# Moving activations placed 32 bytes past a 64-byte boundary in a two-block model kernel

## The chip, the cores and the metric

The kernel runs as one program on one core of a Trainium2 chip. The metric is the device time of one execution in microseconds (us); less is better. All inputs lie in the chip's memory (HBM) at the start, and the output is written there.

## The reference, cut to what matters

Two blocks of two layers each run over 256 tokens of width 1024. The first block mixes an mLSTM and a retention, the second a convolution and a banded attention, followed by a dense feed-forward in layer 0 and eight experts in layer 1. The products with the large weights are what the change touches:

```python
p = h @ w_in[l]                                   # first block, 9 pieces a head, 4 heads
y = jnp.concatenate([y_m, y_r], -1) @ w_out[l]    # 2048 -> 1024
...
proj = h @ w_in_2[l]                              # second block
y = jnp.concatenate([y_conv, y_att], -1) @ w_out_2[l]
f = (jax.nn.silu(h @ w_gate) * (h @ w_up)) @ w_down            # layer 0: 1024 -> 2816 -> 1024
out = out + combine[:, e:e+1] * swiglu(t, w_gate[e], w_up[e], w_down[e])   # layer 1: 8 experts, 1024 -> 3584 -> 1024
```

All of it is float32, and the kernel keeps nearly that precision by splitting each operand into a high and a low part.

## The kernel before, in words

**Units.** The weights come in units of 1 MB: a tile of 128 partitions by 2048 float32. [...] TensorE then takes three products for each 128x128 piece: high weights with the high activations, high with low, low with high. `whi` and `wlo` have three slots each, `raw` has three or six.

**Which operand moves.** A matmul holds one operand in the array (the stationary one, brought by a weight load, at most 128 columns) and streams the other past it (the moving one). `mm(out, a, b)` holds `a` and moves `b`. In the first four stages the weights are stationary and 256 columns of activations move: `products` (L1127 to L1129) and `first_products` (L1144 to L1159) move `hhi` and `hlo`; `rows_product` (L1182 to L1184) moves the halves of y or of the feed-forward's activations (`yhi`/`ylo`, `y2hi`/`y2lo`, `fhi`/`flo`). `token_products` (L1168 to L1170) is the other way round: 128 columns of `hhi` or `hlo` are stationary and 256 columns of weights move. In the experts (L1641 to L1643 and L1670 to L1672) the tokens (`xghi`, `xglo`, `thi`, `tlo`) are stationary and 512 columns of weights move. The gates' sums (L1336 to L1338) hold 36 columns of `ghi` or `glo`, whose slices lie 144 bytes apart, and move `hhi` and `hlo`. Some small matmuls (norm sums L1199, means over a head L1282, scores, transposes) work on plain float32.

**Where tensors lie.** `sb(name, shape, ...)` takes memory in the order in which the program asks for it, and each tensor begins at the next multiple of 32 bytes (per partition) behind the one before. Several stages share one region: an `ExitStack` (`b1`, `b2`, `bf`, `bm`) is closed after its tensors are placed, and the next stage begins at the same address. Read from the built program, the byte address within a partition is a multiple of 64 for `raw`, `whi`, `wlo`, `h`, `hhi`, `hlo`, `yhi`, `ylo`, `y2hi`, `y2lo`, `fhi`, `flo`, `thi`, `tlo`, `xghi`, `xglo`, `pick`, `qpad`, `rot` and `ghi`. It is 32 past such a multiple for `ones`, `mean256`, `zacc`, `q2`, `v2`, `pT` and `mean512`. Slices of the large tensors begin at multiples of 512 bytes inside them.

**What sets the order.** Each engine's instructions are written out by hand and the engines wait for one another by semaphores; there is no scheduler. TensorE goes unit by unit. Beside the units of the first stages the kernel loads 1 MB pieces of the modulation weights (`ada`), which VectorE sums by itself (L1794); the sum's last step is on TensorE (L1211), and SP's next load of that kind waits for it.

Of the kernel before, what the change touches and what calls it, by code (L numbers as in the profile page):

```python
# [5 lines left out]
F32 = mybir.dt.float32  # L6
# [6 lines left out]
P = 128  # L13
# [45 lines left out]

UW = 2048
RAW = 6
HALF = 3
MOE_SLOTS = (3, 4, 5, 2, 0, 1)
# [11 lines left out]
HEAD_UNITS = 9  # L76
OUT1_UNITS = D_INNER * D // (P * UW)
MIX_UNITS = (2 * D_CONV + 3 * D_ATT) // 256
OUT2_UNITS = D * D // (P * UW)

# [16 lines left out]
S_MOE = S_B3 + UNIT_L2  # L97
assert S_MOE % HALF == 2 and A_MIX1 + ADA_MIX[1] == ADA_UNITS and (2 * HEAD_UNITS) % HALF == 0 and JOB_UNITS % RAW == 0 and JOB_UNITS % HL == 0 and ADA_TURN[0] % HALF == 0 and ADA_TURN[1] % HALF == 0
FREE0, DONE0 = HALF, 1
# [25 lines left out]
class Unit:  # L125
# [17 lines left out]
    @property  # L143
    def raw(self):
        return self.n % HALF if self.n < S_MOE else MOE_SLOTS[(self.n - S_MOE) % RAW]

    @property
    def loads(self):
        slots = HALF if self.n < S_MOE else RAW
        if self.n < S_MOE:  # L150
            first = self.n // HALF
        else:
            first = (self.n - S_MOE) // RAW + ((S_MOE + HALF - 1 - self.raw) // HALF if self.raw < HALF else ADA_UNITS // HALF - sum(HALF + i % HALF == self.raw for i in ADA_SPARE))
        return self.turn * (16 * self.per // slots) + (16 * first + 16) if self.per else 16 * first + 16
# [98 lines left out]
def two_block_model(nc, x, positions, consts, c, w_ada, b_ada, norm_g, w_in, conv_w, conv_b, b_igate, b_fgate,  # L253
# [7 lines left out]
    with ctx:  # L261
        def sb(name, shape, dt=F32, stack=ctx):
            return stack.enter_context(nc.sbuf_tensor(name, shape, dt))

        def sem(name):
            return ctx.enter_context(nc.semaphore(name))

        raw = sb("raw", [P, RAW, UW])
        whi = sb("whi", [P, HL, UW], F32R)  # L270
        wlo = sb("wlo", [P, HL, UW], F32R)
        xT = sb("xT", [P, KD, S])
        h = sb("h", [P, KD, S])
        hhi = sb("hhi", [P, KD, S], F32R)
        hlo = sb("hlo", [P, KD, S], F32R)
        cst = sb("cst", [P, C_BEFORE])
        ones = sb("ones", [P, S])
        mean256 = sb("mean256", [P, P])
# [11 lines left out]
        rstd = sb("rstd", [P, S])  # L290
        acc = sb("acc", [P, HALF, S])
        acc2 = sb("acc2", [P, S])

        b1 = ExitStack()
# [44 lines left out]
        sb("before_ylo", [P, D_INNER // P * S], F32, by)  # L340
        spare = sb("spare", [P, 2, UW], F32, by)
        by.close()
# [38 lines left out]

        bm = ExitStack()
        thi = sb("thi", [P, FE // P, P], F32R, bm)
        tlo = sb("tlo", [P, FE // P, P], F32R, bm)
        htok = sb("htok", [P, 2, D], F32, bm)
# [36 lines left out]

        raw_in = [sem(f"raw_in{i}") for i in range(RAW)]
        c_in, rows1_in = sem("c_in"), sem("rows1_in")
# [2090 lines left out]
```

How the kernel before makes its waits and increments, by code:

```python
    def wait(self, back=0):  # L240
        v = self.n - back
        self.eng.wait_ge(self.sem, self.turn * self.per + v if self.per else v)
# [254 lines left out]
        @block.sync  # L497
# [6 lines left out]
            def load(u, src, k):  # L504
                sp.wait_ge(raw_free, u.free(1 - (HALF if u.n < S_MOE else RAW)))
                sp.dma_start(raw[:, u.raw, :].rearrange("p (k n) -> p k n", k=k), src).then_inc(raw_in[u.raw], 16)
# [1 line left out]
            def ada_load(a, block, l, at):  # L509
                if a.n >= ADA_START:
                    sp.wait_ge(ada_done, a.count(1 - HALF))
                elif a.n >= HALF:
                    sp.wait_ge(ada_done, a.n - HALF - len(ADA_SPARE) + 1)
                w = (w_ada, w_ada_2)[block][l].rearrange("(k p) n -> p k n", p=P)
                sp.dma_start(raw[:, a.raw, :].rearrange("p (k n) -> p k n", k=KD), w[:, :, bass.ds(at * 256, 256)])\
                    .then_inc(raw_in[a.raw], 16)
# [58 lines left out]
                        w, c, half = (wg, wu)[j % 4 // 2], j // 4, j % 2  # L575
                        load(u, w[:, 4 * half:4 * half + 4, 512 * c:512 * c + 512], 4)
                    else:
                        f = 2 * (j - JOB_UP)
                        load(u, wd[:, f:f + 2, :], 2)
            sp.wait_ge(ada_done, ADA_UNITS)
            with sp.Fori(0, NE) as e:
                job_loads(e, e, S_MOE, range(JOB_UNITS))
            sp.wait_ge(jobs_ready, 1)
            nx = sp.value_load(jobs[0:1, 0:1], min_val=0, max_val=3)
            with sp.If(nx > 0):
                with sp.Fori(0, nx) as j:
```

## Time and profile before

| | us |
|---|---|
| median of 3 runs | 2150.38 (2146.89 to 2151.61) |
| the profiled execution, device time | 2151.25 |
| its span in the trace | 2149.4 |
| TensorE busy (PE) | 2096.3 |
| VectorE busy (DVE) | 1753.4 |
| ScalarE busy (ACT) | 1321.3 |

The profiled execution is 0.9 us above the median, and 1.9 us of it lie outside its span. On TensorE the start of a matmul is recorded and its end is modelled, and matmuls overlap in the pipeline; the time from the start of one to the start of the next (its spacing) is what a stream of them costs. The busy time of PE only says that something was under way.

### The profile page before, as it was taken

To read this page: it belongs to the slowest core of one execution; us is meant where nothing else is said; L and a number is where in the kernel's file an instruction comes from. 1 tells how busy PE (TensorE), PEld (TensorE's weight loads), DVE (VectorE), ACT (ScalarE), POOL (GpSimd) and SP (SyncE) were. 2 spreads that over 40 slices of the span, in tenths; PEclk is the share of its full clock that TensorE was granted. 3 is DMA by queue.
4 is the path that set the end of the run, shared out by engine and by line. 5 is a ranking of instruction groups with operands and counts; after the bars stand their busy time and mean duration, and the time that the engine had idled before them with its cause. 6 is when DMAs were issued, how large, how long until landed. Compare 5 with 4: busy or idle time off the path is not lost.

```text
span 2149.4 us, 33810 instructions
## 1 busy us (share of the span) xinstructions
PE 2096.3 (98%) x13585; PEld 1866.9 (87%) x13585; DVE 1753.4 (82%) x2161; ACT 1321.3 (61%) x1265; POOL 30.9 (1%) x60
## 2 busy tenths in 40 slices
PE   7999999999999999999999999999999999999998
PEld 5899999899999889999987888888888888888887
DVE  3978875877767878887877988888888888889887
ACT  3565554566645753434656777777777677776775
POOL 3000000000000000000000000000000000000000
PEclk8999999999999999999998999999999999999999
DMA  9777855666656548987545999999999999999995
GB/s 318 239 218 226 247 188 163 198 191 213 184 189 223 189 138 281 288 303 265 177 170 205 369 353 347 374 358 343 361 350 380 345 345 357 362 366 344 360 348 197
DMA packets 356161, 595.07 MB, mean 277 GB/s; under 512 B 10376, under 2 KB 201368, under 8 KB 356008
## 3 DMA queue, kind: packets, MB, share of 16 engines
q1 hardware_dynamic: 352864, 586.92, 79.1%
q0 software_dynamic: 2752, 5.86, 1.2%
q8 instruction: 110, 1.80, 0.3%
q14 instruction: 43, 0.35, 0.0%
q10 hardware_dynamic: 392, 0.13, 0.0%
HBM read 591.80 MB, written 4.22 MB: 277 GB/s over the span
## 4 chain that ended last, share of the span: by engine, by line
PE 82%; DVE 8%; DMA 3%; ACT 3%; issue 3%; SPq 0%; POOL 0%; DVEq 0%; POOLq 0%
PE ps L1641 9%; PE ps L1643 9%; PE ps L1642 9%; PE ps L1127 5%; PE ps L1128 5%; PE ps L1129 5%; PE ps L1670 5%; PE ps L1671 5%; PE ps L1672 5%; PE ps L1182 3%; PE ps L1183 3%; PE ps L1184 3%; DVE acc L1794 2%; DVE wlo L1738 2%; ACT whi L707 1%
## 5 line engine op out<-in xcount | busy, mean ns | idle before, releaser
L1738 DVE TENSOR_TENSOR wlo<-raw,whi 128x2048 fp32r<-128x2048 f32 x485 | 1109.0, 2288 | 264.9 <-ACT whi L707 249.5
L707 ACT CAST whi<-raw 128x2048 fp32r<-128x2048 f32 x485 | 926.0, 1909 | 389.0 <-PE ps L1643 133.7
L1127 PE MATMUL ps<-hhi,whi 128*128 128x256 f32 x1360 | 393.4, 289 | 0.2
L1128 PE MATMUL ps<-hlo,whi 128*128 128x256 f32 x1360 | 385.9, 284 | 0.0
L1129 PE MATMUL ps<-hhi,wlo 128*128 128x256 f32 x1360 | 385.8, 284 | 0.0
L1641 PE MATMUL ps<-whi,xghi 128*128 128x512 f32 x896 | 360.4, 402 | 0.8 <-DVE wlo L1738 0.8
L1643 PE MATMUL ps<-wlo,xghi 128*128 128x512 f32 x896 | 350.1, 391 | 0.0
L1642 PE MATMUL ps<-whi,xglo 128*128 128x512 f32 x896 | 349.0, 390 | 0.0
L1127 PEld LDWEIGHTS ps<-hhi,whi 128*128 128x128 f32 x1360 | 262.1, 193 | 7.3 <-issue 7.0
L1128 PEld LDWEIGHTS ps<-hlo,whi 128*128 128x128 f32 x1360 | 262.1, 193 | 0.3
L1129 PEld LDWEIGHTS ps<-hhi,wlo 128*128 128x128 f32 x1360 | 261.9, 193 | 0.0
L1643 PEld LDWEIGHTS ps<-wlo,xghi 128*128 128x128 f32 x896 | 168.2, 188 | 36.7
L1641 PEld LDWEIGHTS ps<-whi,xghi 128*128 128x128 f32 x896 | 168.3, 188 | 34.2 <-DVE wlo L1738 1.2
L1642 PEld LDWEIGHTS ps<-whi,xglo 128*128 128x128 f32 x896 | 168.6, 188 | 33.7
L1670 PE MATMUL ps<-whi,thi 128*128 128x512 f32 x448 | 175.3, 391 | 0.0
L1671 PE MATMUL ps<-whi,tlo 128*128 128x512 f32 x448 | 174.5, 390 | 0.0
L1672 PE MATMUL ps<-wlo,thi 128*128 128x512 f32 x448 | 174.4, 389 | 0.0
L1794 DVE SCALAR_TENSOR_TENSOR acc<-raw,cact,acc 128x256 f32<-128x256 f32 x324 | 132.7, 478 | 0.0
L1672 PEld LDWEIGHTS ps<-wlo,thi 128*128 128x128 f32 x448 | 84.1, 188 | 17.7
L1670 PEld LDWEIGHTS ps<-whi,thi 128*128 128x128 f32 x448 | 84.2, 188 | 16.8
L1671 PEld LDWEIGHTS ps<-whi,tlo 128*128 128x128 f32 x448 | 84.2, 188 | 16.6
L1168 PE MATMUL ps<-whi,hhi 128*128 128x256 f32 x320 | 92.3, 289 | 0.0
(398 smaller groups left out, 3029.8 us busy)
## 6 DMA issues: line engine op xcount, KB each, us to landing
raw<-in_moe_w_gate_dram SPq DMA_DIRECT2D x112, 1024.0 KB, 6.1
raw<-in_moe_w_up_dram SPq DMA_DIRECT2D x112, 1024.0 KB, 6.1
raw<-in_moe_w_down_dram SPq DMA_DIRECT2D x112, 1024.0 KB, 5.0
raw<-in_w_in_dram SPq DMA_DIRECT2D x92, 1024.0 KB, 5.6
raw<-in_w_ada_dram SPq DMA_DIRECT2D x69, 1024.0 KB, 7.8
raw<-in_w_out_dram SPq DMA_DIRECT2D x24, 1024.0 KB, 5.0
raw<-in_ffn_w_gate_dram SPq DMA_DIRECT2D x11, 1024.0 KB, 9.1
raw<-in_ffn_w_up_dram SPq DMA_DIRECT2D x11, 1024.0 KB, 8.3
```

Of the source, the lines that this page charges most:

```text
L707: nc.scalar.copy(whi[:, u.hl, :], raw[:, u.raw, :]).then_inc(hi_ready, 1)
L1127: mm(ps2[u.bank][:, j], whi[:, u.hl, w], hhi[:, k], start=k == 0, stop=False)
L1128: mm(ps2[u.bank][:, j], whi[:, u.hl, w], hlo[:, k], start=False, stop=False)
L1129: last = mm(ps2[u.bank][:, j], wlo[:, u.hl, w], hhi[:, k], start=False, stop=k == KD - 1)
L1641: mm(o, xghi[:, k, x], whi[:, u.hl, w], start=k == 0, stop=False)
L1642: mm(o, xglo[:, k, x], whi[:, u.hl, w], start=False, stop=False)
L1643: last = mm(o, xghi[:, k, x], wlo[:, u.hl, w], start=False, stop=k == KD - 1)
L1670: mm(o, thi[:, f], whi[:, u.hl, w], start=f == 0, stop=False)
L1671: mm(o, tlo[:, f], whi[:, u.hl, w], start=False, stop=False)
L1672: last = mm(o, thi[:, f], wlo[:, u.hl, w], start=False, stop=f == FE // P - 1)
L1738: V.tensor_tensor(wlo[:, u.hl, :], raw[:, u.raw, :], whi[:, u.hl, :].bitcast(F32), ALU.subtract).then_inc(raw_free, 1)
L1794: last = V.scalar_tensor_tensor(sums[k % 2], w[:, k], cact[:, block, k:k + 1], sums[k % 2], ALU.mult, ALU.add)
```

## The change

Four tensors of 32 bytes are placed between the others. Nothing reads or writes them, and no instruction is added, removed or moved on any engine: line numbers apart, each engine's list of instructions is the same before and after.

```diff
@@ -59,6 +59,7 @@
 UW = 2048
+HALF_LINE = 8
 RAW = 6
@@ -271,8 +272,11 @@
         wlo = sb("wlo", [P, HL, UW], F32R)
         xT = sb("xT", [P, KD, S])
         h = sb("h", [P, KD, S])
+
+        sb("half_line_h", [P, HALF_LINE])
         hhi = sb("hhi", [P, KD, S], F32R)
         hlo = sb("hlo", [P, KD, S], F32R)
+        sb("half_line_c", [P, HALF_LINE])
         cst = sb("cst", [P, C_BEFORE])
@@ -290,6 +294,7 @@
         acc = sb("acc", [P, HALF, S])
         acc2 = sb("acc2", [P, S])
+        sb("half_line_y", [P, HALF_LINE])
 
 
         b1 = ExitStack()
@@ -381,6 +386,7 @@
         bm = ExitStack()
+        sb("half_line_t", [P, HALF_LINE], F32, bm)
         thi = sb("thi", [P, FE // P, P], F32R, bm)
         tlo = sb("tlo", [P, FE // P, P], F32R, bm)
         htok = sb("htok", [P, 2, D], F32, bm)
```

The addresses that follow, as the remainder by 64 bytes:

| tensors | before | after |
|---|---|---|
| `raw`, `whi`, `wlo`, `xT`, `h`, `cst`, `acc`, `rstd` | 0 | 0 |
| `hhi`, `hlo` | 0 | 32 |
| `yhi`, `ylo`, `y2hi`, `y2lo`, `fhi`, `flo` | 0 | 32 |
| `thi`, `tlo`, `xghi`, `xglo`, `htok`, `mg`, `ma`, `pick` | 0 | 0 |
| `qpad`, `qacc`, `rot`, `qk`, `vtok`, `osig`, `zsil`, `bcs`, `arg`, `sT`, `ghi`, `glo`, `fg`, `fa` | 0 | 32 |
| `zacc`, `sig`, `q2`, `rs2`, `v2`, `bias2`, `s2`, `p2`, `pT`, `mean512` | 32 | 0 |
| `ones`, `mean256` | 32 | 32 |

## Rows read from the trace of the kernel before

**Rows 1.** The page: busy time by engine, and the chain that ended last.
```profile
PE 2096.3 (98%) x13585; PEld 1866.9 (87%) x13585; DVE 1753.4 (82%) x2161; ACT 1321.3 (61%) x1265; POOL 30.9 (1%) x60
...
PE 82%; DVE 8%; DMA 3%; ACT 3%; issue 3%; SPq 0%; POOL 0%; DVEq 0%; POOLq 0%
```

**Rows 2.** Busy time by stage: first block, mixer, feed-forward, mixer, experts.
```profile
core 0: us, PE busy (x) PEld busy (x) DVE busy (x) ACT busy (x) POOL busy (x), PEclk, DMA share, GB/s
54.00:358.20 304.20, 294.39 (x2307) 285.99 (x2305) 238.29 (x417) 165.64 (x198) 9.63 (x18) 0.98 0.71 221
363.30:669.00 305.70, 301.77 (x2373) 294.13 (x2374) 227.63 (x371) 170.99 (x206) 0.00 (x0) 0.98 0.62 196
674.70:793.40 118.70, 118.31 (x1140) 104.73 (x1141) 101.94 (x208) 75.83 (x125) 0.80 (x1) 1.00 0.57 184
798.50:1004.10 205.60, 203.61 (x1681) 202.62 (x1682) 175.77 (x296) 82.08 (x67) 0.00 (x0) 0.99 0.85 285
1009.20:1127.90 118.70, 118.22 (x1109) 105.17 (x1110) 98.23 (x195) 75.05 (x123) 0.46 (x1) 0.99 0.51 173
1150.00:2142.00 992.00, 989.05 (x4532) 819.04 (x4531) 863.89 (x550) 709.38 (x479) 0.00 (x0) 1.00 0.97 347
```

**Rows 3.** Groups of matmuls by line and shape: count, busy us, mean ns.
```profile
L1127 PE MATMUL ps<-hhi,whi 128*128 128x256 f32 x1360 | 393.4, 289 | 0.2
...
L1641 PE MATMUL ps<-whi,xghi 128*128 128x512 f32 x896 | 360.4, 402 | 0.8 <-DVE wlo L1738 0.8
...
L1168 PE MATMUL ps<-whi,hhi 128*128 128x256 f32 x320 | 92.3, 289 | 0.0
...
L1182 PE MATMUL ps<-yhi,whi 128*128 128x256 f32 x256 | 73.1, 286 | 0.0
...
L1182 PE MATMUL ps<-fhi,whi 128*128 128x256 f32 x176 | 50.5, 287 | 0.0
...
L1182 PE MATMUL ps<-y2hi,whi 128*128 128x256 f32 x128 | 37.0, 289 | 0.0
...
L1144 PE MATMUL ps<-hhi,whi 128*128 128x256 f32 x64 | 18.6, 320 | 7.9 <-ACT hhi L744 7.9
```

**Rows 4.** Timeline, feed-forward: start us, duration; 24 matmuls apart.
```profile
955.11 0.28 PE L1183 MATMUL ps<-flo,whi 128*128 128x256 f32 x1
...
957.99 0.28 PE L1183 MATMUL ps<-flo,whi 128*128 128x256 f32 x1
```

**Rows 5.** Timeline, experts: 12 matmuls apart.
```profile
1399.91 0.39 PE L1643 MATMUL ps<-wlo,xghi 128*128 128x512 f32 x1
...
1402.63 0.39 PE L1643 MATMUL ps<-wlo,xghi 128*128 128x512 f32 x1
```

**Rows 6.** Timeline, gates' sums: matmuls 1, 19, 23 and the one after 24.
```profile
53.98 0.28 PE L1336 MATMUL ps<-hhi,ghi 128*36 128x256 f32 x1
...
56.09 0.28 PE L1336 MATMUL ps<-hhi,ghi 128*36 128x256 f32 x1
...
56.54 0.28 PE L1337 MATMUL ps<-hlo,ghi 128*36 128x256 f32 x1
...
56.77 0.28 PE L1168 MATMUL ps<-whi,hhi 128*128 128x256 f32 x1
```

**Rows 7.** Timeline, plain float32: a norm's sums, and the first matmul after them.
```profile
668.86 3.61 PE L1199 MATMUL ps<-h,gsq 128*128 128x256 f32 x16
672.31 0.38 PE L1204 MATMUL ps<-gsq,ones 128*128 128x256 f32 x1
```

**Rows 8.** Timeline, plain float32: means over a head, each with its follower.
```profile
94.76 1.03 PE L1282 MATMUL ps<-qpad,mean 128*128 128x256 f32 x4
95.44 0.47 PE L1127 MATMUL ps<-hhi,whi 128*128 128x256 f32 x1
...
322.78 1.02 PE L1282 MATMUL ps<-rot,mean 128*128 128x256 f32 x4
323.45 0.47 PE L1182 MATMUL ps<-yhi,whi 128*128 128x256 f32 x1
```

**Rows 9.** Waits: TensorE up to 1130 us; ScalarE in the feed-forward.
```profile
PE ps L1211 <- DVE acc L1797: 9.6, 5, 3.9
...
ACT whi L707 <- DMA raw<-in_ffn_w_down_dram: 30.6, 7, 6.5
ACT whi L707 <- DMA raw<-in_ffn_w_up_dram: 23.4, 9, 4.8
```

**Rows 10.** Groups of VectorE with one shape: tensors at 0 and at 32.
```profile
L1794 DVE SCALAR_TENSOR_TENSOR acc<-raw,cact,acc 128x256 f32<-128x256 f32 x324 | 132.7, 478 | 0.0
L2112 DVE SCALAR_TENSOR_TENSOR zacc<-zpad,taps,zacc 128x256 f32<-128x256 f32 x150 | 64.6, 477 | 0.0
```

## The prediction

> **What bounds the kernel now.** I read the page first. TensorE has something under way in 98% of the span, and 82% of the chain that ended last is TensorE's; VectorE is busy in 82% and ScalarE in 61% [rows 1]. The table by stage says the same of each part: PE is busy in 294 to 302 of 304 to 306 us in the two layers of the first block, in 118 of 119 us in the mixers, in 204 of 206 us in the feed-forward and in 989 of 992 us in the experts [rows 2]. So the span is nearly the sum of the spacings of TensorE's instructions, and what such a change can be worth is read from these spacings, not from busy times.
>
> The timeline gives them. In the feed-forward, 24 matmuls of 256 moving columns start within 957.99 - 955.11 = 2.88 us: **120.0 ns each** [rows 4]. [...] And float32r matmuls with a small stationary operand of 36 columns take 2.79 us / 24 = 116.3 ns, and in the shortest stretch 0.45 us / 4 = 112.5 ns [rows 6]; the moving operand is the same `hhi` and `hlo` there. [...] I read this as the two reads getting into each other's way, which can depend on where the two operands lie. No float32r row of this trace has its moving operand 32 past a multiple of 64, so whether it does is what I can't read off.
>
> **The change part by part.** No instruction changes, so all cost lies in spacings and durations.
>
> *Matmuls that move activations.* L1127 to L1129 are 3 x 1360 = 4080; L1182 to L1184 are 3 x (256 + 176 + 128) = 1680; the six lines of the first products are 6 x 64 = 384 [rows 3]. With 48 of the very first unit and 48 of the gates' sums that is 6240. Their moving side goes from 0 to 32, the stationary one stays at 0 (except the gates'). The bounds of a relief: at most down to the excess of plain float32, 106.7 + 2.3 = 109.0 ns, that is 11.0 ns or 68.6 us over 6240; or down to the shortest stretch seen, 112.5 ns, that is 7.5 ns or 46.8 us; or nothing. [...] I take 111 ns, between both, nearer the row that exists: 9 ns.
>
> *What of it reaches the end.* The feed-forward has 33 units of 48 = 1584 of them, 14.3 us at 9 ns out of 205.6 us. There ScalarE waits for the DMA of the units 30.6 + 23.4 us [rows 9], the DMA share is 0.85 at 285 GB/s, and VectorE is busy 175.8 us [rows 2]. A stage of 191 us would need 306 GB/s, less than the 347 of the experts [rows 2]; but its slack gets thin, and I count half, 7 us. The other 4656 give 41.9 us. VectorE has 66 and 78 us to spare in the first block's layers, and 17 and 20 in the mixers [rows 2]. TensorE waits for VectorE's `acc` 9.6 us already [rows 9], and that wait ends when it ends, so some of the gain before it is lost: I count 95%, 40 us.
>
> *Matmuls that hold activations.* The 3 x 320 = 960 of L1168 to L1170 [rows 3] get their stationary side at 32 and keep the moving one at 0; the 128 of the experts' gathering too. [...] The gates' sums hold slices at all offsets of 16 bytes and come out at 112.5 ns in the one stretch and at 2.11 us / 18 = 117.2 ns in the rest of them before it [rows 6], so this side seems to matter little. I take 0, between -10 and +3 us.
>
> *The experts.* Tokens and weights keep their remainders; 3 x 896 + 3 x 448 matmuls stay at 226.7 ns. 0 us. Their 992 us are 46% of the span, and no part of the gain is there.
>
> *Everything else that shifts.* VectorE's operation on `acc` (at 0) takes 478 ns, the same one on `zacc` (at 32) 477 [rows 10]. Plain float32 matmuls with the moving operand 12 bytes past a boundary (`qpad`) take 0.68 us for four with the switch, against 0.67 for `rot` at 0 [rows 8]. 0 us for both, on either side of nothing by 2 us at most: 10 ns over some 200 matmuls.
>
> Sum against the profiled execution: 2151.3 - 7 - 40 = **2104 us**; against the median, which is 0.9 us lower, 2103.5. I say 2104.
>
> [...]
>
> **The rivals.**
>
> *The two sides do not depend on a 32-byte shift* (no change, 2151). [...] Against it: 36 columns give 112.5 in one stretch and 116.3 on average [rows 6], with nothing else different. Chance 0.20.
>
> [...] Chance 0.14 for slower in all, mostly well below this price.
>
> *The relief comes, but another engine takes over* (2122). At 11 ns on paper, VectorE's 238 of 304 us in the first layer become 238 of about 287 (83%), and 176 of 188 in the feed-forward (94%) [rows 2]; there the chain would run through DMA, cast and low part for each unit. With nothing from the feed-forward and 70% of the other 41.9 us it ends at 2122. For it: the waits for DMA already there [rows 9]. Against it: each load of `ada` waits for TensorE and starts earlier when TensorE is faster. Chance 0.18.
>
> **How the numbers follow.** The forecast (relief of 7 to 11 ns that mostly reaches the end, 2082 to 2115) has 0.48, the rival with an engine in the way 0.18, no change 0.20, slower 0.14. The first two make the kernel faster: 0.66. For its own case the range is 2082 to 2116. For 8 in 10 it has to reach past no change: 2084 to 2156 leaves out most of the slower case and the full relief of both sides at once (2151 - 69 - 10). A change within 0.2% (4.3 us) can't be told from none; over 6240 matmuls that is 0.7 ns each.
>
> **What would show it.** In the profile after: the 24 matmuls of the feed-forward should take about 2.66 us instead of 2.88, with the experts at 226.7 ns as before. The layers of the first block should be about 14 us shorter each, the mixers about 5 us each, the feed-forward 7 to 14 us, and the experts the same. If the spacing is 120.0 again, the reading of a clash is wrong, or it does not depend on these 32 bytes. [...] If it is near 110 and the stages don't shrink, the waits of TensorE for VectorE and DMA have grown by the difference.

## The result: 2162.3 us, slower by 0.6%

The changed kernel takes 2162.32 us (median of 5, 2158.85 to 2164.33) against 2150.24 for the one before (5 runs). The ratio is 1.0058, with a 95% interval of 1.0046 to 1.0071. The prediction was 2104 us, and faster.

The page of the changed kernel hardly tells it. TensorE, VectorE and ScalarE have nearly the same shares, and so has the chain [rows 1]:

```profile
PE 2105.1 (97%) x13585; PEld 1857.3 (86%) x13585; DVE 1753.6 (81%) x2161; ACT 1321.9 (61%) x1265; POOL 30.9 (1%) x60
...
PE 82%; DVE 10%; issue 3%; ACT 3%; DMA 2%; SPq 0%; POOL 0%; DVEq 0%; POOLq 0%
```

The stages say where to look. Busy time by stage of the changed kernel, cut at the same instructions as in [rows 2] but for the last window, which is a little wider (line numbers have moved on by 6):

```profile
core 0: us, PE busy (x) PEld busy (x) DVE busy (x) ACT busy (x) POOL busy (x), PEclk, DMA share, GB/s
54.00:360.20 306.20, 292.59 (x2308) 283.52 (x2307) 238.10 (x417) 165.56 (x198) 9.49 (x18) 0.98 0.70 220
365.20:667.20 302.00, 297.75 (x2373) 290.18 (x2374) 227.77 (x371) 171.19 (x206) 0.00 (x0) 0.98 0.62 198
672.80:791.20 118.40, 117.35 (x1141) 103.62 (x1142) 102.06 (x208) 76.50 (x126) 0.92 (x1) 1.00 0.56 185
796.00:998.80 202.80, 201.27 (x1680) 200.04 (x1681) 175.71 (x296) 82.50 (x68) 0.00 (x0) 0.99 0.86 288
1003.80:1122.20 118.40, 117.22 (x1108) 104.15 (x1109) 98.39 (x195) 75.16 (x123) 0.62 (x1) 0.99 0.51 173
1144.00:2154.00 1010.00, 1007.83 (x4528) 820.39 (x4527) 863.85 (x549) 709.25 (x479) 0.00 (x0) 1.00 0.96 341
```

| from the norm that opens a stage to the next | before, us | after, us | |
|---|---|---|---|
| start and first block, layer 0 | 358.2 | 360.2 | +2.0 |
| first block, layer 1 | 310.7 | 307.0 | -3.7 |
| mixer 0 | 124.6 | 124.0 | -0.6 |
| feed-forward | 210.6 | 207.7 | -2.9 |
| mixer 1 | 123.8 | 123.4 | -0.4 |
| router, experts, output | 1021.5 | 1039.6 | +18.1 |
| span | 2149.4 | 2161.9 | +12.5 |

Up to the experts 5.7 us are gained in this execution, and the experts, in which I expected nothing to change, lose 18.1. The spacings say the same per matmul. Timeline of the changed kernel, in order: `hhi` moving (24 matmuls apart), the feed-forward's activations moving (24 apart), the experts (12 apart):

```profile
900.67 0.28 PE L1133 MATMUL ps<-hhi,whi 128*128 128x256 f32 x1
...
903.47 0.28 PE L1133 MATMUL ps<-hhi,whi 128*128 128x256 f32 x1
...
965.12 0.28 PE L1189 MATMUL ps<-flo,whi 128*128 128x256 f32 x1
...
968.00 0.28 PE L1189 MATMUL ps<-flo,whi 128*128 128x256 f32 x1
...
1401.53 0.40 PE L1649 MATMUL ps<-wlo,xghi 128*128 128x512 f32 x1
...
1404.32 0.39 PE L1649 MATMUL ps<-wlo,xghi 128*128 128x512 f32 x1
```

`hhi` moves at 2.80 / 24 = 116.7 ns instead of 120.0; the feed-forward's activations at 2.88 / 24 = 120.0, no faster than in [rows 4]; the experts' weights at 2.79 / 12 = 232.5 instead of 226.7 [rows 5]. Averaged over all matmuls of a kind (start to start, waits and stretches at the lower clock left out), L1127 to L1129 went from 119.9 to 116.8 ns, L1168 to L1170 from 119.9 to 118.3, L1182 to L1184 stayed at 119.9, and the experts' went from 228.2 to 232.8 (gate and up) and from 227.2 to 232.4 (down).

The tokens kept their remainder by 64, but not by 256. In the kernel before, every large float32r tensor, weights too, lies 128 past a multiple of 256. In the changed one the tokens lie at 0, so 128 from the weights; `hhi` and `hlo` lie 32 ahead of the weights, the activations of y and of the feed-forward 96 ahead. (Addresses are read from the built programs.) That gave theory A: what counts is the distance between the moving and the stationary operand, over 256 bytes. Its rival B: only the remainder by 64 counts, and something else slowed the experts.

### The profile page after: what moved, and what is told of

Its sections match the earlier page's. It is cut to its first block, busy times and chain, and to the rows that moved or that the text cites. A ratio compares the mean times of both kernels' runs of the same rounds, so it can differ in the third digit from the quotient of the medians.

```text
span 2161.9 us, 33810 instructions
## 1 busy us (share of the span) xinstructions
PE 2105.1 (97%) x13585; PEld 1857.3 (86%) x13585; DVE 1753.6 (81%) x2161; ACT 1321.9 (61%) x1265; POOL 30.9 (1%) x60
## 4 chain that ended last, share of the span: by engine, by line
PE 82%; DVE 10%; issue 3%; ACT 3%; DMA 2%; SPq 0%; POOL 0%; DVEq 0%; POOLq 0%
PE ps L1649 9%; PE ps L1647 9%; PE ps L1648 9%; PE ps L1133 5%; PE ps L1134 5%; PE ps L1135 5%; PE ps L1678 5%; PE ps L1676 5%; PE ps L1677 5%; PE ps L1188 3%; PE ps L1189 3%; PE ps L1190 3%; DVE wlo L1744 2%; DVE acc L1800 2%; PE ps L1622 1%
## 5 line engine op out<-in xcount | busy, mean ns | idle before, releaser
L1133 PE MATMUL ps<-hhi,whi 128*128 128x256 f32 x1360 | 388.1, 285 | 0.5 <-DVE wlo L1744 0.5
L1134 PE MATMUL ps<-hlo,whi 128*128 128x256 f32 x1360 | 380.0, 279 | 0.0
L1135 PE MATMUL ps<-hhi,wlo 128*128 128x256 f32 x1360 | 379.9, 279 | 0.0
L1648 PE MATMUL ps<-whi,xglo 128*128 128x512 f32 x896 | 353.5, 395 | 0.0
L1133 PEld LDWEIGHTS ps<-hhi,whi 128*128 128x128 f32 x1360 | 256.6, 189 | 7.6 <-issue 7.3
L1134 PEld LDWEIGHTS ps<-hlo,whi 128*128 128x128 f32 x1360 | 256.5, 189 | 0.3
L1135 PEld LDWEIGHTS ps<-hhi,wlo 128*128 128x128 f32 x1360 | 256.1, 188 | 0.0
```

The source lines that it names most:

```text
L1133: mm(ps2[u.bank][:, j], whi[:, u.hl, w], hhi[:, k], start=k == 0, stop=False)
L1134: mm(ps2[u.bank][:, j], whi[:, u.hl, w], hlo[:, k], start=False, stop=False)
L1135: last = mm(ps2[u.bank][:, j], wlo[:, u.hl, w], hhi[:, k], start=False, stop=k == KD - 1)
L1648: mm(o, xglo[:, k, x], whi[:, u.hl, w], start=False, stop=False)
```

## The experiments

### The distance, measured by itself

A kernel that leaves the model out and runs TensorE alone, in the kernel's order of three products. Each line is one pair of places (two of the lines are shown):

```diff
+ for o, h, l, a, b, f, e in run(256, 32, 0): mm(o, h, a, **f); mm(o, h, b, **c); last = mm(o, l, a, **e)
+ for o, h, l, a, b, f, e in run(512, 128, 0): ...      # columns, moving shift, stationary shift in bytes
```

> This kernel leaves the whole model out: it copies x to the output and runs TensorE alone, 144 float32r matmuls in a row for each pair of places (the moving operand shifted by m bytes, the stationary one by s, from the same remainder by 512), in the kernel's own pattern of three, with nothing else reading or writing the memory. Theory A, the spacing depends on the difference of the two places by 256 bytes: difference 0 gives 120 ns at 256 columns and 227 at 512, 32 gives 117, 96 gives 120 to 121, 512 columns with a difference of 128 give 232, and 256 and 512 bytes repeat 0; equal shifts of both repeat 0. Theory B, the spacing depends on the difference by 64 bytes alone, and what slowed the experts is another thing (the other engines or the DMAs): 64, 128 and 192 repeat 0, also at 512 columns. Theory C, a fixed price: 120 and 227 everywhere.

Timeline of this kernel, each pair 96 matmuls apart: 256 columns with distance 0 (L58), 32 (L60) and 192 (L66), then 512 columns with distance 0 (L71) and 128 (L77):

```profile
33.42 0.28 PE L58 MATMUL ps<-mhi,shi 128*128 128x256 f32 x1
...
44.94 0.28 PE L58 MATMUL ps<-mhi,shi 128*128 128x256 f32 x1
...
67.80 0.28 PE L60 MATMUL ps<-mhi,shi 128*128 128x256 f32 x1
...
79.00 0.28 PE L60 MATMUL ps<-mhi,shi 128*128 128x256 f32 x1
...
169.85 0.28 PE L66 MATMUL ps<-mhi,shi 128*128 128x256 f32 x1
...
180.76 0.28 PE L66 MATMUL ps<-mhi,shi 128*128 128x256 f32 x1
...
254.88 0.40 PE L71 MATMUL ps<-mhi,shi 128*128 128x512 f32 x1
...
276.66 0.39 PE L71 MATMUL ps<-mhi,shi 128*128 128x512 f32 x1
...
454.68 0.40 PE L77 MATMUL ps<-mhi,shi 128*128 128x512 f32 x1
...
477.08 0.40 PE L77 MATMUL ps<-mhi,shi 128*128 128x512 f32 x1
```

That is 11.52 / 96 = 120.0 ns, 11.20 / 96 = 116.7, 10.91 / 96 = 113.6, 21.78 / 96 = 226.9 and 22.40 / 96 = 233.3. The whole map, from the last 119 gaps of each 144 matmuls:

| moving ahead of stationary, bytes | 0 | 16 | 32 | 48 | 64 | 96 | 128 | 160 | 192 | 224 | 256 | 512 |
|---|---|---|---|---|---|---|---|---|---|---|---|---|
| 256 columns, ns | 120.0 | 118.6 | 116.7 | 118.3 | 117.8 | 120.0 | 118.7 | 117.4 | 113.3 | 118.3 | 120.0 | 120.0 |
| 512 columns, ns | 226.7 | 231.6 | 233.3 | 233.3 | 228.9 | 233.4 | 233.4 | 234.3 | 233.3 | 233.3 | 226.7 | 226.7 |

Moving the stationary operand on by 64 gives what 192 gives (113.3 and 233.4), and by 32 what 224 gives (118.4 and 233.3). By 128 it gives 118.7 and 232.4, at 512 columns 1.0 ns less than the moving operand's 128; that is the one place of the map where the distance alone doesn't give the number. Both shifted by 32, or both by 128, give 120.0 and 226.7 again. So the spacing follows the distance, it repeats after 256 bytes, and it does so with nothing but TensorE at work. Theory A holds. B falls: 64, 128 and 192 are alike by 64 and read 117.8, 118.7 and 113.3. The fixed price (C) falls too. The changed kernel's own values at 256 columns stand in this table: 116.7 for 32 (116.8 there), 120.0 for 96 (119.9), and 118.3 for 224, which is the distance of L1168 to L1170, where the weights move and `hhi` is held (118.3).

### The tokens put back, and the tokens alone

```diff
 # on the changed kernel
-        sb("half_line_t", [P, HALF_LINE], F32, bm)
+        sb("half_line_t", [P, 104], F32, bm)
```

> The changed kernel with 416 bytes instead of 32 ahead of the experts' tokens, so that they lie at the same remainder by 512 as the weights again, as before the change; the activations of the earlier stages stay at 32 and 96 past it. Theory A: the experts' spacing returns from 232.5 to 227 ns and the kernel takes 2162 - 18 = 2144 us, some 6 us less than the one before. Theory B: nothing changes, 2162 us.

Measured: 2142.49 us, ratio to the kernel before 0.9966 (0.9953 to 0.9980). The experts' matmuls are back at 227.5 and 228.0 ns.

```diff
 # on the kernel before
         bm = ExitStack()
+        sb("half_line_t", [P, 32], F32, bm)
```

> The kernel before with 128 bytes ahead of the experts' tokens and nothing else: they lie 128 past the weights' remainder by 256, as in the changed kernel. Theory A: the experts take 18 to 20 us more, 2169 us. Theory B: 2150 us as before.

Measured: 2166.63 us, ratio 1.0085 (1.0059 to 1.0110). (All tensors of the experts' stage move by these 128 bytes, not the tokens alone; that the tokens' place is enough rests on the map.) Timeline of this kernel, experts, 12 apart:

```profile
1401.64 0.40 PE L1644 MATMUL ps<-wlo,xghi 128*128 128x512 f32 x1
...
1404.44 0.40 PE L1644 MATMUL ps<-wlo,xghi 128*128 128x512 f32 x1
```

2.80 / 12 = 233.3 ns here, 232.6 to 232.8 on average. The two runs show it from both sides: 128 bytes between tokens and weights cost 16 us (2166.6 against 2150.4) to 20 us (2162.3 against 2142.5), and the activations' new places are worth 8 (2142.5 against 2150.4, with an interval of 4 to 10).

### Finer places, and the experts' own order

> The model is left out again; TensorE alone, 144 matmuls for each set of places. It refines the first map, where a moving operand 192 bytes ahead of the stationary one (by 256) took 113.3 ns at 256 columns and every difference but 0 (by 256) took 229 to 234 ns at 512. Theory A (each read is cut into pieces of the memory, and pieces that fall on one another in time cost): around 192 the spacing rises within 8 to 16 bytes on either side, the low and the high part have to be placed alike, and in the experts' order of three (moving high, moving low, moving high) 0 stays the best at 512 columns. Rival: 192 is a chance of this one pattern and the experts' order has another best place, under 226 ns.

The kernel is that of the first map with other places. At 256 columns: 176 gives 119.3, 184 gives 120.0, 188 gives 118.6, 192 gives 113.3, 196 gives 121.7, 200 gives 120.0, 208 gives 119.2 ns. Four bytes to either side undo it. With only the high or only the low moving operand at 192 it is 119.3 and 117.8, and with both at 192 but the low stationary operand moved on by 64 or 192 it is 118.2 and 117.8. In the experts' order the same 192 gives 117.8 too. At 512 columns in the experts' order (moving high, low, high is now moving high, high, low): 0 gives 226.7, 4 gives 236.7, 8 gives 233.3, 16 gives 231.7, 64 gives 228.9, 128 gives 232.4, 240 gives 236.6, 252 gives 226.7. The 232.4 for 128 is the changed kernel's own average. The first map had 233.4 and 232.4 for 128, and single units of the kernel with the tokens alone run at 233.3, so the last nanosecond is not a matter of the order of products only. No place tried is better than 0. That the spacing rises on either side of 192 held; the rival (a better place for the experts) fell. The pieces of the memory, from which theory A had it, no run shows.

### All activations at 192, all activations at 32

```diff
 # on the kernel before: 48 and 16 columns for 192 bytes; 8 and 56 for 32 bytes
+        sb("ahead_h", [P, 48])
         hhi = sb("hhi", [P, KD, S], F32R)
...
         bm = ExitStack()
+        sb("ahead_t", [P, 16], F32, bm)
         thi = sb("thi", [P, FE // P, P], F32R, bm)
```

> The kernel before with 192 bytes ahead of hhi and 64 ahead of the experts' tokens: all moving activations of the first stages lie 192 bytes past the weights' remainder by 256, tokens and weights stay alike. Theory A: the spacing of the 6240 matmuls falls from 120.0 to 113.3 ns, that of the 960 with stationary activations to 117.8, the experts stay at 227; 41.8 + 2 us on paper. In the changed kernel only about half of the 15 us saved on spacings reached the end; with that half the time is 2128, with 95% of it 2108 us. Rival (what counts is a place at an odd multiple of 32 bytes): 192 is a multiple of 64, so nothing changes, 2150.

> The kernel before with 32 bytes ahead of hhi and 224 ahead of the experts' tokens: all moving activations lie 32 bytes past the weights' remainder by 256, those of y and of the feed-forward too (96 in the changed kernel), tokens and weights alike. Theory A: 116.7 ns in all 6240, 227 in the experts; 5 us less than the run with the tokens put back (2142), 2138 us. If it is the remainder by 64 alone that counts, 2142.

Measured: 2137.52 us, ratio 0.9936 (0.9919 to 0.9952), and 2138.01 us, ratio 0.9941 (0.9924 to 0.9957). Both beat the kernel before and the changed one. The second is as expected: y and the feed-forward's activations, at 32 instead of 96, move at 116.7 to 117.7 ns on average (by stage) instead of 119.9, and the kernel takes 4.5 us less than with the tokens put back. The intervals of the two runs, some 3 us each, are nearly as wide as this step. The first misses its time, in part because it misses its spacing: `hhi` moves at 115.7 ns on average and y and the feed-forward's activations at 117.4, not at 113.3. Its timeline shows why. Two units of the feed-forward, each 24 matmuls apart:

```profile
889.85 0.28 PE L1129 MATMUL ps<-hhi,whi 128*128 128x256 f32 x1
...
892.57 0.28 PE L1129 MATMUL ps<-hhi,whi 128*128 128x256 f32 x1
...
902.28 0.28 PE L1129 MATMUL ps<-hhi,whi 128*128 128x256 f32 x1
...
905.11 0.28 PE L1129 MATMUL ps<-hhi,whi 128*128 128x256 f32 x1
```

2.72 / 24 = 113.3 ns in the one unit, 2.83 / 24 = 117.9 in the other. Of the 85 units of L1129 to L1131, 43 run at 113.3 and 42 at 117.7 to 117.8 in their second half; none lies between.

### What picks the rhythm of a unit

```diff
+ ahead(kind)     # 0: nothing; 1: one float32 matmul of 128 columns; 2: two of one column; 3: eight of 256
  for ... in run(kind, 256, 192, 192, 0, 0): ...                      # 48 matmuls
```

> The model is left out; TensorE alone in units of 48 matmuls like the kernel's, each place of the moving operand (0 to 224 bytes ahead of the stationary one) begun in four ways: straight on, behind one plain float32 matmul of 128 columns, behind two of one column, behind eight of 256. Then all 64 combinations of places of the two moving and of the low stationary operand in steps of 64. Theory A2 (the stream falls into a rhythm, and how a unit begins picks it where there is more than one): at 192 some beginnings give 113.3 and others 117.8 ns for the whole unit, as in the full kernel's units; 0 has one rhythm of 120.0 whatever the beginning; the difference decides which rhythms there are. Rival (the place alone decides): each place has one spacing whatever the beginning, and the 117.8 ns in the full kernel come from the other engines' accesses, which are absent here.

Timeline of this kernel, distance 192, 24 matmuls apart: begun straight on (L88), and behind two matmuls of one column (L90):

```profile
184.40 0.28 PE L88 MATMUL ps<-mhi,shi 128*128 128x256 f32 x1
...
187.12 0.28 PE L88 MATMUL ps<-mhi,shi 128*128 128x256 f32 x1
...
196.02 0.28 PE L90 MATMUL ps<-mhi,shi 128*128 128x256 f32 x1
...
198.85 0.28 PE L90 MATMUL ps<-mhi,shi 128*128 128x256 f32 x1
```

113.3 and 117.9 ns for the same operands. Straight on or behind one matmul of 128 columns the unit runs at 113.3, behind two of one column or eight of 256 at 117.8. One of the later units with this same placement began behind eight of 256 and ran at 113.3, so it is something finer than the kind of the beginning. At distance 0 every beginning gives 120.0, at 64 every one 117.8. The change's own 32 has two rhythms as well: 117.8 straight on, 116.6 to 116.7 behind the other three. Theory A2 holds and the rival falls: the place decides which rhythms there are, the beginning which one a unit falls into. Of the 64 combinations of high and low places, only two went below 115 (both 113.3), both with the two moving operands at 192.

### How much of a shorter spacing reaches the end

In the changed kernel the shorter spacings are worth 3.1 ns x 4080 + 1.6 ns x 960 + 2.5 ns x 384 (the first products, 119.8 to 117.3) = 15.1 us on paper, but the experts start only 5.7 us earlier. That 5.7 is one execution against one, and such a difference is uncertain by some 3 us: the kernel with the tokens alone moved, which differs from the kernel before in nothing that runs before the experts, starts them at 1125.1 us, 2.8 earlier than it. By the medians of several executions the same placement (tokens put back) is worth 7.8 us, half of the 15.1.

TensorE's waits up to 1130 us (total, times, longest) in the kernel before, where only one line is new:

```profile
PE ps L1276 <- DVE sT L2032: 4.9, 4, 1.8
```

and in the changed one, where the first two lines answer to L1211 [rows 9] and L1144 [rows 3]:

```profile
PE ps L1217 <- DVE acc L1803: 9.4, 4, 4.1
PE ps L1150 <- ACT hhi L750: 7.9, 4, 2.2
PE ps L1282 <- DVE sT L2038: 7.7, 4, 2.4
```

The waits for `acc` and `hhi` are the same, those for `sT` have grown from 4.9 to 7.7 us, the longest from 1.8 to 2.4. And they have a second price. Windows of 27 and 26 us with one of these waits in each, the kernel before and then the changed one (columns as in [rows 2]):

```profile
145.00:172.00 27.00, 25.20 (x203) 24.73 (x202) 22.55 (x43) 11.58 (x11) 0.53 (x1) 1.00 0.64 197
274.00:300.00 26.00, 24.19 (x195) 23.72 (x194) 21.56 (x42) 11.79 (x11) 0.53 (x1) 1.00 0.60 189
```

```profile
145.00:172.00 27.00, 24.64 (x188) 23.86 (x187) 20.95 (x40) 11.09 (x11) 0.61 (x1) 0.94 0.56 176
274.00:300.00 26.00, 23.64 (x180) 22.80 (x179) 19.92 (x38) 12.10 (x12) 0.53 (x1) 0.93 0.53 170
```

The granted clock of both stretches is 1.00 in the kernel before, and 0.94 and 0.93 in the changed one. There a part of each, which begins at about the end of the longer pause, has a granted clock of 0.50 (windows 151.6 to 154.8 and 281.3 to 284.5 us). By these shares I estimate the cost at 0.06 x 27 = 1.6 us of work, and 0.07 x 26 = 1.8. The timeline is close to that: from the first matmul behind the pause (L1276, now L1282) to the next weights' first (L1127, now L1133) the kernel before takes 1.99 us at both places, the changed one 3.47 and 3.66. The fall is there too, at the same two places, with the tokens put back (0.94 and 0.93). The pause goes before the fall but doesn't settle it: in the kernel with all activations at 192 the two pauses are 2.40 us each, and the clock falls at the second (0.50 from 279.3 to 282.4 us) and not at the first, which ends at 151.35 us (1.00 over 145 to 172).

To see whether VectorE is the cause, its sums were made light in both placements. Six of the eight steps of each sum take 8 columns instead of 256, so these kernels leave most of the modulation's sums out (VectorE's busy time falls from 1753.4 to 1673.9 us in the first of them):

```diff
-   last = V.scalar_tensor_tensor(sums[k % 2], w[:, k], ...)
+   last = V.scalar_tensor_tensor(sums[k % 2][:, 0:8], w[:, k, 0:8], ...)
```

> The kernel before, with VectorE's six later steps of each modulation sum (L1794, 324 instructions) over 8 columns instead of 256, so that the modulation values are not those of the model; the base for the next run. VectorE has about 100 us less to do in the first four stages, some of TensorE's waits for it end sooner, and the experts start a few us earlier than at 1128 us. The spacings stay at 120.0 and 227 ns.

> The same lighter sums in the kernel with the activations placed as in the change and the tokens back at the weights' remainder. The spacings before the experts sum to 15 us less, as there. Theory W (what the spacings save is partly spent again in waits for VectorE and in the clock that falls during them): with a light VectorE nearly all of it reaches the experts' start, 13 to 15 us against the run before this one. Rival (the other half goes into TensorE's own changes of operand kind, whatever VectorE does): 6 us, as between the two full kernels (1127.9 and 1122.7).

Measured: 2136.16 and 2124.11 us, 12.1 apart; in their profiled executions the experts start at 1109.7 and 1099.4 us, 10.3 apart. With the full sums the same two placements are 7.8 us apart by their medians. Windows of the second of the two light kernels:

```profile
145.00:172.00 27.00, 27.00 (x221) 26.63 (x221) 20.96 (x41) 14.48 (x18) 1.05 (x2) 1.00 0.77 243
274.00:300.00 26.00, 26.00 (x216) 25.79 (x216) 21.24 (x41) 13.89 (x17) 1.05 (x2) 1.00 0.53 180
```

TensorE is busy throughout, at 1.00. So these two pauses, and the falls of the clock behind them, are VectorE's lateness: they are gone with the light sums. How much of the missing gain they explain is less sure. Of 15 us on paper some 8 arrive with the full sums and 12 without, but each of these differences is uncertain by about 3 us, so the 4 us between them is hardly clear of noise. Theory W expected 13 to 15 at the experts' start, the rival 6; the measured 10.3 lies between and decides for neither, and the last 3 to 5 us stay open. The times go with the clock: the ten executions with the tokens put back run from 2137.7 us (mean granted clock 0.989) to 2147.9 (0.983), and the traced one is the slowest of them.

## Why the prediction was wrong, step by step

Without it the change gains 8 us (2142.5), far from the 47 of my sum, which the next two steps explain. I read the full addresses and reduced them by 64 before thinking about them. No rival touched the experts, which are nearly half of the span, so this case had no chance at all in my numbers.

**"I take 111 ns, between both"** for the 6240 moving activations was too good. `hhi` and `hlo` came to 116.8, 3.1 ns instead of 9; y and the feed-forward's activations stayed at 120.0, because three pads in a row had put them 96 ahead and not 32. I treated as one place what was two. The gain on paper was 15 us, not 56.

**"I count 95%" and "I count half, 7 us"** for what reaches the end were too much: 5.7 of 15.1 us in the changed kernel's profile, 38%, and about half by the medians. The waits for VectorE that I listed, 9.6 us [rows 9], were only those for `acc`; the ones for `sT` grew by 2.8 us, and the clock fell behind two of them. The rest of the shortfall stays open.

**Matmuls that hold activations**: I took 0 with bounds of -10 and +3, both estimates of mine (the -10 from the same 109.0 ns) that no run shows; they gained 1.6 ns each (119.9 to 118.3), 1.5 us. **Everything else that shifts**: I took 0, and VectorE's busy time is 1753.6 us against 1753.4 and ScalarE's 1321.9 against 1321.3. Right, as far as these two engines go; the waits that grew are counted above.

**The rivals.** Neither no change nor an engine in the way (ScalarE's cast of `raw` to `whi` at L707, VectorE's `wlo` at L1738) describes it. For the slower one I had in mind that a moving read with its start at 32 costs more by itself. No run shows that: with both operands at 32 the spacings are 120.0 and 226.7, as with both at 0. The time was slower for a reason that was not on the list.

## What to carry to other kernels

Where float32r matmuls with 128 stationary columns follow one another, look at the distance between the moving and the stationary operand over 256 bytes, not at each one's own alignment, and measure it for the number of columns in use: 192 helps at 256 columns (113.3 for 120.0 ns) and harms at 512 (233.3 for 226.7). A pad ahead of one tensor moves all that are placed behind it, so write down the addresses of every pair that meets in a matmul, in all stages, before and after. And of a saving on the busiest engine a part can go into its next waits: here about half did not arrive.

## What the runs showed that I had not expected

A stream of matmuls falls into a rhythm and keeps it: the same 48 matmuls run at 113.3 or at 117.8 ns each, by how they were begun. (The map's columns are thus each one rhythm of their place, not always the only one.) Four bytes matter (192 gives 113.3, 196 gives 121.7; at 512 columns 0 and 252 give 226.7, 4 gives 236.7). Why 256 bytes are the period, and why equal places are the best at 512 columns and among the worst at 256, no run here tells.
